# Where TensorE waits for the overflow words of a mixture of experts, and where the last tile keeps its high parts

## The chip, the core and the metric

The kernel runs on one core of one Trainium2 chip. The metric is the device time of a whole execution, in microseconds (us). The engines of the core are named as in the profile: PE is TensorE (matrix products), DVE is VectorE, ACT is ScalarE, POOL is GpSimd (which also issues DMAs and the gathers by index), SP is SyncE (which only issues DMAs here). Each engine runs its own list of instructions in order; they meet only at semaphores, which one engine or a DMA raises and another waits for.

## The reference

A decoder trunk of two layers on 512 tokens of width 1024. Each layer mixes tokens (state space, latent attention and block attention side by side, one output projection) and then runs a mixture of experts. The change lies in the experts alone:

```python
def moe_ffn(x, router_w, router_bias, w_gate, w_up, w_down):
    scores = sigmoid(t @ router_w)                  # 512 tokens, 16 experts
    ...                                             # best group of 4 experts, then the top 2 in it
    for e in range(N_EXPERTS):                      # D_MODEL 1024, D_EXPERT 512
        hid = silu(t @ w_gate[e]) * (t @ w_up[e])
        out = out + gates[:, e:e + 1] * (hid @ w_down[e])
```

The data are float32 throughout.

## The kernel before, in words

A loop over the two layers (`with nc.Fori(0, DEPTH) as L`) holds one block with a program for each engine. Each layer has the same course: norm and input projection, the mixers, the output projection, the router, then the experts, and at the end the rows of the experts are gathered back and added to x.

**Routing.** The router's scores are turned into a table: for every expert one tile of up to 128 token slots, and up to `NOV` = 7 further tiles for experts with more tokens. 17 tiles (`NTL`) always run; the rest depend on the data. PE makes the table with 8 small matmuls (L1025), DVE copies it to integers (`slot_idx`, L1844), and POOL then gathers the tokens of tile 0 and tile 1 from DRAM by these indices (L2057). DVE goes on for some twenty short steps: the places of the rows (`pos_i`), the weights of the two choices (`w12`), and last the control words `ctl` (L1863), which say how many further tiles there are and of which experts. Each of `pos_i` and `ctl` raises the semaphore `pos_dn` by one. The control words are read at the end of the 17 tiles by PE, ACT, DVE and POOL (`value_load`), and by SP for the expert of the last fixed tile.

**PE between routing and experts.** PE waits for `pos_dn` to be 2, runs `keep_warm(28)`, which is 28 matmuls of an identity into a bank that nobody reads (L781; a float32 matmul of this kind leaves two records in the trace, so 56), then turns the tokens of tile 0 (`turn_x(0, 0)`, L1034, which waits for the gather), runs `keep_warm(5)` and starts `gate_up(0)`.

**The tiles.** For every tile PE runs `gate_up` (L1048 to L1050, two products of 24 matmuls), `turn_x` of the next tile, `down` of the tile before (L1071 to L1077, 20 matmuls), and `turn_h` (L1056, which turns the hidden rows). A float32 product is made of three faster ones: weights and tokens are split into a high part (rounded by ACT: L1338 for gate and up, `down_hi`, L1377, for down) and a low part (what is left, by DVE: L1751, and `down_lo`, L1905, which writes it over the raw weights in their slot). The high parts of down live in `biasm` and `gain` (`down_hi_parts`), one set of buffers for all tiles; so `down_hi(e)` waits until `down(e - 1)` has read them (`y_ps`, 2e). The high parts of gate and up live in `mod` from column 0 to 5120 and in `actT` (`hi_parts`); they are free when `gate_up(e)` has finished (`gu_ps`, 2e + 2). Of `mod`, columns 5120 to 6144 hold the modulation that `y_out` multiplies with, and columns 0 to 2048 are loaded anew by SP behind the last `gate_up` (L717).

**The last tile (16).** PE runs `gate_up(16)`, `down(15)`, `turn_h(16)`, `down(16)`. Beside it ACT runs `silu(16)` (L1365), `h_out(16)` (L1369, L1370: the turned hidden rows out of PSUM), `down_hi(16)`; DVE runs `hidden(16)` (L1872), `y_out(15)` (L1879, two halves), `hidden_low(16)` (L1898), `down_lo(16)` (L1905, two parts) and `y_out(16)`. `down(16)` waits for `h_out`, `hidden_low`, both parts of `down_lo`, `y_out(15)` and the loaded weights. The weights of down of tile 16 are issued by SP (L684) when `down(14)` has ended.

## Time and profile before

| | us |
|---|---|
| median of 3 runs (lowest, highest) | 1593.85 (1592.6, 1597.31) |
| the profiled execution: its own time | 1589.72 |
| the profiled execution: its span, first to last instruction | 1587.7 |
| PE busy | 1382.0 (87%) |
| DVE busy | 1097.7 (69%) |
| ACT busy | 720.3 (45%) |
| POOL busy | 186.0 (12%) |
| mean granted TensorE clock | 0.916 of full speed |

Starts in the trace are counted from the first instruction. Busy times overlap, so they say only which engine is used most; which wait counts is read in each stage from the rows of the trace. The granted clock is given as a share of 2.4 GHz: 1.00 is 2.4 GHz and 0.50 is 1.2 GHz, and a value between them is the mean of a stretch that holds both. The first layer's experts run from about 463 to 788 us, the second layer's from about 1231 to 1556 us.

### The profile page before, as it was taken

To read this page: it belongs to the slowest core of one execution; us is meant where nothing else is said; L and a number is where in the kernel's file an instruction comes from. 1 tells how busy PE (TensorE), PEld (TensorE's weight loads), DVE (VectorE), ACT (ScalarE), POOL (GpSimd) and SP (SyncE) were. 2 spreads that over 40 slices of the span, in tenths; PEclk is the share of its full clock that TensorE was granted. 3 is DMA by queue.
4 is the path that set the end of the run, shared out by engine and by line. 5 is a ranking of instruction groups with operands and counts; after the bars stand their busy time and mean duration, and the time that the engine had idled before them with its cause. 6 is when DMAs were issued, how large, how long until landed. Compare 5 with 4: busy or idle time off the path is not lost. (4 is left out here: it accounts for less than half of the span.)

```text
span 1587.7 us, 17407 instructions
## 1 busy us (share of the span) xinstructions
PE 1382.0 (87%) x6479; PEld 1074.5 (68%) x6479; DVE 1097.7 (69%) x1295; ACT 720.3 (45%) x983; POOL 186.0 (12%) x268
## 2 busy tenths in 40 slices
PE   7499988987989999999618998888698999999981
PEld 3377785665777777777416777656577777777761
DVE  0577775674559888888358786666646888888862
ACT  1422433454237666666123333344513666666640
POOL 0000013400101000010020000261000100000002
PEclk9699999688999999999858999978799999999995
DMA  9536562321369999997365374243107799999944
GB/s 347 201 106 227 189 226 70 133 80 67 126 266 354 406 394 400 401 401 310 119 229 180 123 274 172 93 159 106 67 33 311 267 398 401 403 402 408 386 154 172
DMA packets 95260, 379.54 MB, mean 239 GB/s; under 512 B 5897, under 2 KB 8695, under 8 KB 85704
## 3 DMA queue, kind: packets, MB, share of 16 engines
q1 hardware_dynamic: 71592, 308.82, 51.5%
q0 software_dynamic: 15264, 55.63, 9.0%
q10 hardware_dynamic: 8320, 13.96, 2.5%
q8 instruction: 54, 0.88, 0.2%
q14 instruction: 30, 0.25, 0.0%
HBM read 345.58 MB, written 32.82 MB: 238 GB/s over the span
## 5 line engine op out<-in xcount | busy, mean ns | idle before, releaser
L1048 PE MATMUL ps<-mod_rounded,work_rounded 128*128 128x512 f32 x340 | 137.7, 405 | 2.0 <-DVE work_rounded L1885 2.0
L1050 PE MATMUL ps<-mod_rounded,work_rounded 128*128 128x512 f32 x340 | 133.8, 394 | 0.0
L1751 DVE TENSOR_TENSOR ring_rounded<-ring,mod_rounded 128x2048 fp32r<-128x2048 f32 (+1 forms) x54 | 102.9, 1930 | 23.5 <-ACT mod_rounded L1338 23.5
L1049 PE MATMUL ps<-ring_rounded,work_rounded 128*128 128x512 f32 x288 | 113.2, 393 | 0.0
L1751 DVE TENSOR_TENSOR work_rounded<-work,mod_rounded 128x2048 fp32r<-128x2048 f32 (+1 forms) x48 | 91.4, 1932 | 31.3 <-ACT mod_rounded L1338 31.3
L1431 DVE SCALAR_TENSOR_TENSOR gain<-ring,csil,gain 128x512 f32<-128x512 f32 x134 | 102.2, 763 | 4.6 <-DMA ring<-in_ada_w 1.6
L1049 PE MATMUL ps<-work_rounded 128*128 128x512 f32 x256 | 100.6, 393 | 0.0
L806 PE MATMUL ps<-ring_rounded,actT_rounded 128*128 128x512 f32 (+1 forms) x256 | 93.5, 365 | 0.0
L1338 ACT ACTIVATE mod_rounded<-ring 128x2048 fp32r<-128x2048 f32 (+1 forms) x54 | 86.2, 1631 | 0.0
L1202 ACT ACTIVATE work<-ps 128x512 f32<-128x512 f32 (+1 forms) x48 | 26.3, 548 | 127.8 <-PE ps L806 76.4
L1075 PE MATMUL ps<-biasm_rounded,work_rounded 128*128 128x512 f32 x136 | 82.2, 604 | 0.0
L1133 ACT ACTIVATE work<-x 128x1024 f32<-128x1024 f32 x16 | 16.9, 1058 | 143.7 <-DVE x L1453 70.0
L1048 PE MATMUL ps<-actT_rounded,work_rounded 128*128 128x512 f32 x204 | 81.0, 397 | 0.0
L1050 PE MATMUL ps<-actT_rounded,work_rounded 128*128 128x512 f32 x204 | 80.2, 393 | 0.0
L1358 ACT ACTIVATE work_rounded<-ps 128x512 fp32r<-128x512 f32 x68 | 36.9, 595 | 92.8 <-PE ps L1034 92.8
L806 PE MATMUL ps<-work_rounded,mod_rounded 128*128 128x512 f32 (+1 forms) x192 | 77.5, 404 | 0.0
L1338 ACT ACTIVATE mod_rounded<-work 128x2048 fp32r<-128x2048 f32 (+1 forms) x48 | 76.6, 1632 | 0.0
L923 PE MATMUL ps<-work 64*128 64x256 f32 (+7 forms) x128 | 63.3, 585 | 14.4 <-DVE sml L1705 12.3
L2057 POOL DMA_INDIRECT work<-ffn_rows,slot_idx x34 | 37.5, 1102 | 318.7 <-PE ps L1034 286.0
L1048 PEld LDWEIGHTS ps<-mod_rounded,work_rounded 128*128 128x128 f32 x340 | 63.7, 187 | 16.2 <-DVE work_rounded L1885 2.9
L1050 PEld LDWEIGHTS ps<-mod_rounded,work_rounded 128*128 128x128 f32 x340 | 63.9, 188 | 15.8
L806 PE MATMUL ps<-work_rounded,actT_rounded 128*128 128x512 f32 (+1 forms) x192 | 72.1, 376 | 0.0
(329 smaller groups left out, 3586.1 us busy)
## 6 DMA issues: line engine op xcount, KB each, us to landing
ring<-in_ada_w SPq DMA_DIRECT2D x38, 1024.0 KB, 5.3
ring<-in_moe_w_gate SPq DMA_DIRECT2D x18, 2048.0 KB, 10.0
ring<-in_moe_w_up SPq DMA_DIRECT2D x18, 2048.0 KB, 10.4
ring<-in_moe_w_down SPq DMA_DIRECT2D x18, 2048.0 KB, 11.3
work<-in_moe_w_gate SPq DMA_DIRECT2D x16, 2048.0 KB, 10.2
work<-in_moe_w_up SPq DMA_DIRECT2D x16, 2048.0 KB, 10.9
work<-in_moe_w_down SPq DMA_DIRECT2D x16, 2048.0 KB, 11.7
expert_rows<-work POOLq DMA_DIRECT2D x34, 512.0 KB, 8.3
```

Source lines behind the costliest of these rows:

```text
L806: mm = pe.matmul(ps[n % 2][:, 0:wd], h_[:, P * t:P * t + P], w_, start=first_, stop=last_)
L923: pe.matmul(ps[2 + n % 2][:, 0:P * (t + 1)], qT[0:d, h % 2, P * t:P * t + P], kT[0:d, h % 2, 0:P * (t + 1)], start=True, stop=True).then_i ...
L1048: pe.matmul(ps[j][:, :], xl, hi, start=k == 0, stop=False)
L1049: pe.matmul(ps[j][:, :], xh, lo, start=False, stop=False)
L1050: mm = pe.matmul(ps[j][:, :], xh, hi, start=False, stop=k == KD - 1)
L1075: pe.matmul(ps[6 + b][:, :], hT_lo[:, k, :], hi_[:, k - k0, cols], start=False, stop=False)
L1202: a.activation(dst, ps[n % 2][:, 0:in_width[b]], ACT.Silu if b == 0 else ACT.Copy).then_inc(win_ev, 1)
L1338: a.activation(buf, slots[3 * odd + j][:, 512 * k0:512 * k1], ACT.Copy).then_inc(w_hi, 1)
L1358: a.activation(xeT_r[:, 4 * j:4 * j + 4, :], ps[2 + j][:, :].rearrange("p (k n) -> p k n", k=4), ACT.Copy).then_inc(xt_ev, 1)
L1431: add(v.scalar_tensor_tensor(acc, w, csil[:, k:k + 1], acc, ALU.mult, ALU.add))
L1751: v.tensor_tensor(slots_r[3 * odd + j][:, 512 * k0:512 * k1], slots[3 * odd + j][:, 512 * k0:512 * k1], buf.bitcast(F32), ALU.subtract).th ...
L2057: g.indirect_dma_start(out=dst, out_offset=None, in_=hf_rows, in_offset=bass.IndirectOffsetOnAxis(ap=col, axis=0)).then_inc(sem_, 16)
```

## The change

Four edits, all in the experts of each layer.

1. PE: the wait for `pos_dn` leaves its place behind the table matmuls and stands ahead of the `value_load` of the control words, behind `down` of the last tile. ACT gets the same wait ahead of its own `value_load`.
2. PE: `keep_warm(28)` becomes `keep_warm(20)`, and `keep_warm(5)` becomes `keep_warm(4)`.
3. The high parts of down of the last tile go to `mod`, columns 2048 to 4096 and 4096 to 5120 (`down_hi_last`), and no longer to `biasm` and `gain`. `down_hi` of that tile waits for `gu_ps` = 34, the end of `gate_up(16)`, in place of `y_ps` = 32, the end of `down(15)`.
4. The order for the last tile: ACT runs `down_hi(16)` ahead of `h_out(16)`, and DVE runs `down_lo(16)` ahead of `y_out(15)` and `hidden_low(16)`.

```diff
--- before.py
+++ after.py
@@ -226,6 +226,10 @@
 
     DOWN_SPLIT = 3
     down_hi_parts = [(0, 2, biasm_r[:, :, :].rearrange("p a b -> p (a b)")), (2, 3, gain_r[:, :])]
+    down_hi_last = [(0, 2, mod_r[:, 2048:4096]), (2, 3, mod_r[:, 4096:5120])]
+
+    def down_high(e):
+        return down_hi_last if e == NTL - 1 else down_hi_parts
 
     hL = mod_r[:, 2048:6144].rearrange("p (k n) -> p k n", k=KD)
     in_hi = [view(s0 + 2048 * n, 2048, of=work_r) for n in range(3)] + [mod_r[:, 0:2048]]
@@ -1024,7 +1028,6 @@
                 for m in range(2 * T):
                     mm = pe.matmul(ps[3][:, 0:NT], row_oh[:, m, :], tile_tok[:, m, :], start=m == 0, stop=m == 2 * T - 1)
                 mm.then_inc(tab_ps, 1)
-                pe.wait_ge(pos_dn, 2)
 
 
                 def turn_x(e, odd):
@@ -1069,7 +1072,7 @@
                     for b in range(2):
                         cols = slice(512 * b, 512 * b + 512)
                         pe.matmul(ps[6 + b][:, :], hT3, w[:, 3, cols], start=True, stop=False)
-                        for k0, k1, buf in down_hi_parts:
+                        for k0, k1, buf in down_high(e):
                             hi_ = buf.rearrange("p (k n) -> p k n", k=k1 - k0)
                             for k in range(k0, k1):
                                 pe.matmul(ps[6 + b][:, :], hT_lo[:, k, :], hi_[:, k - k0, cols], start=False, stop=False)
@@ -1078,9 +1081,9 @@
                                                start=False, stop=k == DOWN_SPLIT - 1)
                         mm.then_inc(y_ps, 1)
 
-                keep_warm(28)
+                keep_warm(20)
                 turn_x(0, 0)
-                keep_warm(5)
+                keep_warm(4)
                 gate_up(0, 0, first=True)
                 turn_x(1, 1)
                 turn_h(0)
@@ -1092,6 +1095,7 @@
                     turn_h(e)
                 down(NTL - 1, (NTL - 1) % 2)
 
+                pe.wait_ge(pos_dn, 2)
                 nov = pe.value_load(ctl[0:1, 0:1], min_val=0, max_val=NOV)
                 with pe.Fori(0, NOV - 1) as i:
                     with pe.If(nov > i + 1):
@@ -1371,9 +1375,11 @@
 
                 def down_hi(e, odd):
                     a.wait_ge(*expert_loaded(e, odd, 2))
-                    if e:
+                    if e == NTL - 1:
+                        a.wait_ge(gu_ps, 2 * NTL)
+                    elif e:
                         a.wait_ge(y_ps, 2 * e)
-                    for k0, k1, buf in down_hi_parts:
+                    for k0, k1, buf in down_high(e):
                         a.activation(buf, slots[3 * odd + 2][:, 1024 * k0:1024 * k1], ACT.Copy).then_inc(d_hi, 1)
 
                 def expert_turn(e, odd, first=False):
@@ -1388,8 +1394,9 @@
                 for e in range(NTL - 1):
                     expert_turn(e, e % 2, first=e == 0)
                 silu(NTL - 1)
+                down_hi(NTL - 1, (NTL - 1) % 2)
                 h_out(NTL - 1)
-                down_hi(NTL - 1, (NTL - 1) % 2)
+                a.wait_ge(pos_dn, 2)
                 nov = a.value_load(ctl[0:1, 0:1], min_val=0, max_val=NOV)
                 with a.Fori(0, NOV - 1) as i:
                     with a.If(nov > i + 1):
@@ -1899,7 +1906,7 @@
                                     ALU.subtract).then_inc(hl_lo, 1)
 
                 def down_lo(e, odd):
-                    for m, (k0, k1, buf) in enumerate(down_hi_parts):
+                    for m, (k0, k1, buf) in enumerate(down_high(e)):
                         v.wait_ge(d_hi, 2 * e + (m + 1))
                         cols = slice(1024 * k0, 1024 * k1)
                         v.tensor_tensor(slots_r[3 * odd + 2][:, cols], slots[3 * odd + 2][:, cols], buf.bitcast(F32),
@@ -1915,9 +1922,9 @@
                     hidden_low(e)
                     down_lo(e, e % 2)
                 hidden(NTL - 1)
+                down_lo(NTL - 1, (NTL - 1) % 2)
                 y_out(NTL - 2, (NTL - 2) % 2)
                 hidden_low(NTL - 1)
-                down_lo(NTL - 1, (NTL - 1) % 2)
                 y_out(NTL - 1, (NTL - 1) % 2)
                 v.wait_ge(y_ev, 2 * NTL)
                 v.wait_ge(pos_dn, 2)
```

On PE, behind the routing, this stood before (the names in brackets are the semaphores that an instruction waits for: `slot_selectors_done` is `sel_dn`, `positions_done` is `pos_dn`, `tokens_gathered0` is `gat[0]`, `expert_tokens_low_done` is `xl_dn`):

```order
L1025 MATMUL ps<-work_rounded 128x24 [waits slot_selectors_done]
L1025 MATMUL ps<-work_rounded 128x24 x7
L781 MATMUL ps<-cst 128x128 [waits positions_done]
L781 MATMUL ps<-cst 128x128 x27
L1034 MATMUL ps<-cst,work 128x128 [waits tokens_gathered0]
L1034 MATMUL ps<-cst,work 128x128 x7
L781 MATMUL ps<-cst 128x128 x5
L1048 MATMUL ps<-mod_rounded,work_rounded 128x512 [waits weights_low_done,expert_tokens_low_done]
```

and this stands there now:

```order
L1029 MATMUL ps<-work_rounded 128x24 [waits slot_selectors_done]
L1029 MATMUL ps<-work_rounded 128x24 x7
L785 MATMUL ps<-cst 128x128 x20
L1037 MATMUL ps<-cst,work 128x128 [waits tokens_gathered0]
L1037 MATMUL ps<-cst,work 128x128 x7
L785 MATMUL ps<-cst 128x128 x4
L1051 MATMUL ps<-mod_rounded,work_rounded 128x512 [waits weights_low_done,expert_tokens_low_done]
```

The fill of 28 became 20 and follows the table matmuls without a wait; the wait now stands ahead of the load of the control words at the end of the tiles.

On ACT, in the last tile, this stood before, from `silu(16)` to the control words (`hidden_transposed` is `ht_ps`, `expert_out_in_psum` is `y_ps`, `gate_up_in_psum` is `gu_ps`):

```order
L1365 ACTIVATE work<-ps 128x512 [waits hidden_done,gate_up_in_psum]
L1369 ACTIVATE work_rounded<-ps 128x384 [waits hidden_transposed]
L1370 ACTIVATE work<-ps 128x128
L1377 ACTIVATE biasm_rounded<-ring 128x2048 [waits expert_out_in_psum,slot2_loaded]
L1377 ACTIVATE gain_rounded<-ring 128x1024
L1393 TENSOR_LOAD ctl
```

and this stands there now:

```order
L1369 ACTIVATE work<-ps 128x512 [waits hidden_done,gate_up_in_psum]
L1383 ACTIVATE mod_rounded<-ring 128x2048 [waits gate_up_in_psum,slot2_loaded]
L1383 ACTIVATE mod_rounded<-ring 128x1024
L1373 ACTIVATE work_rounded<-ps 128x384 [waits hidden_transposed]
L1374 ACTIVATE work<-ps 128x128
L1400 TENSOR_LOAD ctl [waits positions_done]
```

The two big copies moved ahead of `h_out`, write to `mod`, and wait for `gate_up` where they waited for `down`.

On DVE, in the last tile, this stood before, from `hidden(16)` to the load of the control words (`down_weights_high_done` is `d_hi`, `hidden_columns_out` is `ht_ev`):

```order
L1872 TENSOR_TENSOR work<-ps,work 128x512 [waits hidden_transposed,gate_up_in_psum,gate_silu_done]
L1879 TENSOR_TENSOR work<-ps,mod 128x512 [waits expert_out_in_psum,expert_out_stored1]
L1879 TENSOR_TENSOR work<-ps,mod 128x512 [waits expert_out_in_psum]
L1898 TENSOR_TENSOR work_rounded<-ps,work_rounded 128x384 [waits hidden_columns_out]
L1905 TENSOR_TENSOR ring_rounded<-ring,biasm_rounded 128x2048 [waits down_weights_high_done]
L1905 TENSOR_TENSOR ring_rounded<-ring,gain_rounded 128x1024 [waits down_weights_high_done]
L1879 TENSOR_TENSOR work<-ps,mod 128x512 [waits expert_out_in_psum,expert_out_stored0]
L1879 TENSOR_TENSOR work<-ps,mod 128x512 [waits expert_out_in_psum]
L1924 TENSOR_LOAD ctl [waits positions_done,expert_out_scaled]
```

and this stands there now:

```order
L1879 TENSOR_TENSOR work<-ps,work 128x512 [waits hidden_transposed,gate_up_in_psum,gate_silu_done]
L1912 TENSOR_TENSOR ring_rounded<-ring,mod_rounded 128x2048 [waits down_weights_high_done]
L1912 TENSOR_TENSOR ring_rounded<-ring,mod_rounded 128x1024 [waits down_weights_high_done]
L1886 TENSOR_TENSOR work<-ps,mod 128x512 [waits expert_out_in_psum,expert_out_stored1]
L1886 TENSOR_TENSOR work<-ps,mod 128x512 [waits expert_out_in_psum]
L1905 TENSOR_TENSOR work_rounded<-ps,work_rounded 128x384 [waits hidden_columns_out]
L1886 TENSOR_TENSOR work<-ps,mod 128x512 [waits expert_out_in_psum,expert_out_stored0]
L1886 TENSOR_TENSOR work<-ps,mod 128x512 [waits expert_out_in_psum]
L1931 TENSOR_LOAD ctl [waits positions_done,expert_out_scaled]
```

The two differences of `down_lo(16)` moved ahead of both halves of `y_out(15)` and of `hidden_low(16)`.

## Rows read from the trace of the kernel before

**Rows 1.** Groups of PE by line and form: busy us, mean ns | idle before, releaser.

```profile
L1048 PE MATMUL ps<-mod_rounded,work_rounded 128*128 128x512 f32 x340 | 137.7, 405 | 2.0 <-DVE work_rounded L1885 2.0
...
L781 PE MATMUL ps<-cst 128*128 128x128 f32 x332 | 44.9, 296 | 7.8 <-DVE ctl L1863 7.8
...
L1071 PE MATMUL ps<-ring,work 128*128 128x512 f32 x72 | 38.8, 622 | 12.2 <-DVE ring_rounded L1905 12.2
```

**Rows 2.** Timeline, layer 1, routing to tile 0: start, duration, what [idle before].

```profile
444.51 4.71 PE L781 MATMUL ps<-cst 128*128 128x128 f32 x40
...
449.74 1.06 PE L1025 MATMUL ps<-work_rounded 128*128 128x24 f32 x8 [0.52 <-DVE work_rounded L1839]
...
451.89 1.05 POOL L2057 DMA_INDIRECT work<-ffn_rows,slot_idx  x1 [16.11 <-DVE slot_idx L1844]
...
454.58 2.27 DVE L1751 TENSOR_TENSOR ring_rounded<-ring,mod_rounded 128x2048 fp32r<-128x2048 f32 x1
...
454.72 8.40 PE L781 MATMUL ps<-cst 128*128 128x128 f32 x56 [3.91 <-DVE ctl L1863]
...
462.96 1.04 PE L1034 MATMUL ps<-cst,work 128*128 128x128 f32 x8
```

**Rows 3.** DMA issues of 451.5 to 452.5 us, with median us to landing.

```profile
work<-ffn_rows,slot_idx POOLq DMA_INDIRECT x1, 6.1
```

**Rows 4.** The same, of 1218 to 1219.9 us, layer 2.

```profile
work<-ffn_rows,slot_idx POOLq DMA_INDIRECT x1, 6.6
```

**Rows 5.** Timeline, layer 2, routing to tile 0.

```profile
1219.29 1.05 POOL L2057 DMA_INDIRECT work<-ffn_rows,slot_idx  x1 [16.06 <-DVE slot_idx L1844]
...
1230.64 1.04 PE L1034 MATMUL ps<-cst,work 128*128 128x128 f32 x8
```

**Rows 6.** Stretches: length, busy of PE, PEld, DVE, ACT, POOL, granted clock, DMA share, GB/s.

```profile
455.00:459.00 4.00, 4.00 (x21) 4.00 (x22) 1.86 (x1) 0.00 (x0) 0.00 (x0) 0.54 0.69 273
305.00:308.50 3.50, 3.50 (x13) 2.04 (x11) 2.25 (x5) 1.06 (x2) 3.15 (x5) 0.50 0.00 0
987.50:991.00 3.50, 3.50 (x20) 3.50 (x20) 1.93 (x3) 0.51 (x3) 0.00 (x0) 0.54 0.00 0
```

**Rows 7.** Timeline of PE, mixers of layer 2, ahead of the third stretch.

```profile
986.44 2.49 PE L878 MATMUL ps<-work 128*128 128x64 f32 x16 [1.47 <-DVE work L1627]
```

**Rows 8.** Timeline, layer 1, last tile.

```profile
766.72 1.02 PE L1071 MATMUL ps<-work 128*128 128x512 f32 x2
766.98 0.69 DVE L1872 TENSOR_TENSOR work<-ps,work 128x512 f32<-128x512 f32 x1 [4.89 <-issue]
...
772.78 0.69 DVE L1879 TENSOR_TENSOR work<-ps,mod 128x512 f32<-128x512 f32 x1 [2.17 <-PE ps L1077]
773.22 0.49 ACT L1369 ACTIVATE work_rounded<-ps 128x384 fp32r<-128x384 f32 x1 [11.29 <-PE ps L1056]
...
773.76 1.91 ACT L1377 ACTIVATE biasm_rounded<-ring 128x2048 fp32r<-128x2048 f32 x1
...
773.90 0.56 DVE L1898 TENSOR_TENSOR work_rounded<-ps,work_rounded 128x384 fp32r<-128x384 f32 x1 [0.43 <-ACT work L1370]
775.56 1.06 ACT L1377 ACTIVATE gain_rounded<-ring 128x1024 fp32r<-128x1024 f32 x1
775.70 2.29 DVE L1905 TENSOR_TENSOR ring_rounded<-ring,biasm_rounded 128x2048 fp32r<-128x2048 f32 x1 [1.24 <-ACT biasm_rounded L1377]
777.91 1.22 DVE L1905 TENSOR_TENSOR ring_rounded<-ring,gain_rounded 128x1024 fp32r<-128x1024 f32 x1
...
779.28 2.05 PE L1071 MATMUL ps<-ring,work 128*128 128x512 f32 x2 [6.10 <-DVE ring_rounded L1905]
...
787.18 0.69 DVE L1879 TENSOR_TENSOR work<-ps,mod 128x512 f32<-128x512 f32 x1 [2.17 <-PE ps L1077]
```

**Rows 9.** DMA issues of 755 to 756 us, with us to landing.

```profile
ring<-in_moe_w_down SPq DMA_DIRECT2D x1, 2048.0 KB, 10.7
```

**Rows 10.** Timeline: when that load was issued.

```profile
755.29 0.38 SPq L684 DMA_DIRECT2D ring<-in_moe_w_down  x1
```

## The prediction

> **What bounds the kernel now.** I read the views in this order: the groups of PE, the timeline of the stretch between routing and tile 0, the landing of the gathers, the timeline of the last tile, and the granted clock of a few short stretches. The reader is to see first that between its two ends the expert stage is bound by PE: the first product of a whole gate and up, 340 matmuls over both layers, was kept waiting for 2.0 us in all [rows 1]. So nothing inside the tiles can be won or lost by moving copies on ACT or DVE, and only the stage's two ends are open. Both show as idle time of PE in the same view: 7.8 us at L781 until DVE has written `ctl`, and 12.2 us at L1071 until DVE has made the low weights of down [rows 1]. Two layers share these, 3.9 and 6.1 us each [rows 2, 8]. The change goes for exactly these two waits.
>
> **The start of the experts, layer 1.** PE ends the table matmuls at 449.74 + 1.06 = 450.80, idles 3.91, and then fills from 454.72 to 462.96, when `turn_x(0)` follows without a pause [rows 2]. What `turn_x(0)` really needs is the gather: issued at 451.89, landed 6.1 later, 457.99 [rows 2, 3]. So before, the fill ran 5.0 us past the landing. Now the fill starts at 450.80. Its length: 40 records took 4.71 us where the clock was full [rows 2], and 20 matmuls are 40 records, so it ends at 455.5, before the landing. `turn_x(0)` starts at about 458.1 (a tenth for the release), 4.9 us earlier. In layer 2 the gather lands at 1219.29 + 6.6 = 1225.9, so `turn_x(0)` moves from 1230.64 to 1226.0, 4.6 us earlier [rows 4, 5]. Sum 9.5. What follows hangs on `turn_x(0)` at the same distances: the shorter second fill, 8 records instead of 10, still ends ahead of `xeL`. The cover that stands by: DVE's first low weights are done at 454.58 + 2.27 = 456.85 [rows 2], so DVE is free when `x_low(0)` comes; the steps that write `ctl` keep their time and PE reads `ctl` over 300 us later, so the moved wait costs nothing there, and neither does ACT's. Nobody else is queued behind them.
>
> Here the Trainium skill can be held against a row. The row: this gather took 6.1 us from issue to landing [rows 3]. The page "DMA: Bandwidth & Descriptors", section "Anatomy of one DMA — SWDGE (gpsimd) path", has a fixed 2.0 us and bytes by 436e3 per us; for half a megabyte that makes an estimate of 3.2 us, which the trace doesn't bear out. What it would give is a rival below.
>
> **What the clock takes back at the start.** PE now idles from 455.5 to 458.1, 2.6 us, and in layer 2 about 3.0 (there the gather's issue, 1219.29, again 1.09 behind the end of the table matmuls, puts that end at 1218.2 and the end of the fill at 1222.9). Before, the 3.9 us of idling brought the clock down: it was 0.54 over 455 to 459, during the fill [rows 6], where it hurt nobody. Gaps shorter than the new one do it too: 1.47 us idle ahead of 986.44 was followed by a clock of 0.54 from 987.5 to 991, with PE busy throughout [rows 6, 7]. So I take it that the clock falls in this gap, or just behind it, and that `turn_x`, the small fill and the first products of tile 0 meet half of it. Bounds: zero, if it does not fall; above, what a fallen clock cost a dense `down`: `down(16)` took 787.18 - 779.28 = 7.90 from its first matmul to the release of DVE, `down(15)` 772.78 - 766.72 = 6.06, so 1.84 [rows 8]. The low stretch partly lies in the gap and beside `x_low`'s chain, so I take 1.0 a layer. Start of both layers: 9.5 - 2.0 = 7.5.
>
> **The end of the experts.** Before, from `turn_h(16)`, which ends at 779.28 - 6.10 = 773.18, a chain of five steps kept PE idle: `h_out` 773.22, the first copy of `down_hi` 773.76 to 775.67, DVE's difference 775.70 to 777.99, the second difference to 779.13, PE 779.28 [rows 8]. Now the copies wait for `gate_up(16)` only. It ended when DVE's `hidden` started, 766.98. The other thing they wait for is the load, landed at 755.29 + 10.7 = 765.99, 1 us earlier [rows 9, 10]. So ACT copies from 767.0 to 768.9, and, as the second started 1.80 behind the first, to 769.9. DVE: `hidden` until 767.67, wait, first difference 768.95 to 771.24, second to 772.4. All of this lies beside `down(15)` on PE, 766.72 to 772.6. What is late next: `y_out(15)`, whose second half needs the end of `down(15)`, 772.78, and takes 0.69, so 773.5; `h_out`, unchanged, 773.22 to 773.87; `hidden_low` 773.90 to 774.46. `down(16)` follows 0.15 later, as it did: 774.6 instead of 779.28, 4.7 us earlier. The first half of `y_out(15)` is 2.5 us later than before, which only its own bank feels, and that bank is needed at 774.6. POOL's store of tile 15 waits for both halves and starts up to 0.5 later; its landing is needed by nobody before the last gather.
>
> The clock gives something on top: the gap shrinks from 6.10 to 774.6 - 773.18 = 1.4 us. If the clock stays up, `down(16)` takes 6.06 and not 7.90: 1.84 more. The gap lies just under the 1.47 after which it fell [rows 7], so I count it as staying up in about two of three ends and take 1.2 a layer (bounds 0 and 1.84). The page "TensorE: Matmul & The Clock Gate", section "What's actually happening", says the monitor runs freely and is not started by the kernel, so how many matmuls are slow varies from run to run; the sum would be the same, and it is why this term is a share and not yes or no. End: 2 × (4.7 + 1.2) = 11.8. Behind `down(16)` stand the store, the gathers of the rows and the barrier, all of which hang on it, so the gain goes through to the end of the layer. Layer 2 repeats these rows (12.2 for two waits [rows 1]).
>
> **The sum.** 7.5 + 11.8 = 19.3 us. The profiled execution took 1589.72 (span 1587.7), so it would take 1570.4. The median of the runs is 1593.85, 4 us above the profiled one; 1593.85 - 19.3 = 1574.5, which I give.
>
> **Rivals.**
> - The clock never falls at the new gaps. For it: the same stretches are dense otherwise. Against: rows 6 and 7. Gain 9.5 + 9.4 + 3.7 = 22.6: 1571.3.
> - The gather lands earlier than it did, since the price of 6.1 comes from sharing the queues with the last weight loads, and that share could turn out smaller. At 3.2 after issue it would land at 455.1, within the fill, `turn_x(0)` starts at the end of the fill, 455.5 and 1222.9, and the clock has no gap to fall in. Start 7.5 + 7.7 = 15.2, with the end's 11.8 a gain of 27.0: 1566.9. The page of the skill named above gives the 3.2. Against: nothing that the gather shares is moved by the change.
> - The end gives less, because the load of the last down weights has only 1.0 us of slack now where it had 7.8. If it lands 3 us later in an ordinary run, the differences end at 774.4, `y_out(15)` follows to 775.7 and pushes `hidden_low` to 776.3: `down(16)` at 776.4, gain 2.9 in place of 4.7 and the longer gap drops the clock: 2 × (1.8 + 1.2) = 6 less, 1580.5.
> - The clock stays low for long. From 305 to 308.5 it was 0.50 with PE busy throughout [rows 6]. If it stayed low for some 13 us behind each start, that costs 6.5 a layer in place of 1.0: gain 8.3, 1585.5. For it: that row. Against: that was in the mixers with their small matmuls, and behind the gap in front of `down(16)` it came back within the tile.
> - Slower than before: the same mechanism, in the first tiles of both layers, with its price: each us at half clock costs 0.5 us of PE-bound work. Without the clock's cost the gain is 21.3, so it turns at 43 us of low clock in all, 21 a layer, more than a tile. At 30 us a layer it costs 30: 1602.5. Against: no dense stretch of the rows shows it.
>
> **How the numbers follow.** Forecast 0.73 (own range 1570 to 1579, from the clock bounds and 2 us of scatter of a median); clock never falls 0.13; earlier gather 0.02; late load 0.07; long low clock 0.03; slower 0.02. About 0.3%, 5 us, is what a measurement of this kernel can tell from no change. Faster by more: all but the last two, 0.95; the long low clock can end within it, 0.03; slower 0.02. The range 1567 to 1581.5 leaves out the last two, the earlier gather at its edge, and the rest's own tails.
>
> **What would show it.** After the table matmuls PE must go into 40 records of fill with no idle time, and `turn_x(0)` must begin within 0.2 of the gather's landing, some 7.3 us after the table matmuls' end (before: 12.2). L781 must lose its wait for `ctl`. In the last tile the copies L1377 must start beside `down(15)`, the wait of L1071 must be about 1.4 us and be released by `hidden_low` and no longer by `down_lo`. It is wrong if the wait of L1071 is over 3 us, if the first tile after `turn_x(0)` takes over 3 us longer than before, or if another wait of PE appears in the tiles between.

## The result

| | before | changed |
|---|---|---|
| median (lowest, highest), us, 4 runs each | 1595.58 (1592.6, 1598.45) | 1572.11 (1570.04, 1574.24) |
| profiled execution, its own time | 1589.72 | 1572.55 |
| its span | 1587.7 | 1570.7 |
| mean granted clock | 0.916 | 0.919 |

The ratio changed to before is 0.9874, 95% interval 0.9845 to 0.9903: 1.3% faster, which is 20.1 us by the ratio (15 to 25 by its interval). Forecast were 1574.5 us and a gain of 19.3. The medians are 23.5 us apart and the profiled executions 17.2.

### The profile after

The waits of PE in the expert stage of layer 1, 440 to 800 us (who waited for whom, us in total, times, longest); layer 2 has the same four:

```profile
PE ps L1037 <- DMA work<-ffn_rows,slot_idx: 3.1, 1, 3.1
PE ps L1074 <- DVE work_rounded L1905: 1.4, 1, 1.4
PE ps L1059 <- DVE work L1879: 1.2, 1, 1.2
PE ps L1051 <- DVE work_rounded L1892: 0.5, 1, 0.5
```

The wait for `ctl` (3.9 us a layer, [rows 1]) is gone, and the 6.1 us ahead of `down(16)` have become 1.4, now released by L1905, `hidden_low`. A new wait stands at L1037, `turn_x(0)`: 3.1 us for the gather.

The start of layer 1, to be laid beside [rows 2] (start, duration, what [idle before]):

```profile
451.96 1.06 PE L1029 MATMUL ps<-work_rounded 128*128 128x24 f32 x8 [0.51 <-DVE work_rounded L1846]
...
452.87 4.71 PE L785 MATMUL ps<-cst 128*128 128x128 f32 x40
...
454.11 1.05 POOL L2064 DMA_INDIRECT work<-ffn_rows,slot_idx  x1 [16.11 <-DVE slot_idx L1851]
...
460.71 1.23 PE L1037 MATMUL ps<-cst,work 128*128 128x128 f32 x8 [3.13 <-DMA work<-ffn_rows,slot_idx]
...
461.74 1.92 PE L785 MATMUL ps<-cst 128*128 128x128 f32 x8
...
463.38 0.80 PE L1051 MATMUL ps<-mod_rounded,work_rounded 128*128 128x512 f32 x1
...
464.82 0.46 PE L1051 MATMUL ps<-mod_rounded,work_rounded 128*128 128x512 f32 x1
```

The fill follows the table matmuls without a pause and takes the 4.71 us that 40 records take at the full clock. `turn_x(0)` begins within 0.1 of the gather's landing, which came 6.6 us after its issue here and 6.5 in layer 2:

```profile
work<-ffn_rows,slot_idx POOLq DMA_INDIRECT x1, 6.6
```

The second fill (8 records in 1.92) and the first products (0.80, 0.63) are slow; the product that starts at 465.12 takes the full clock's 0.40.

The last tile of layer 1, beside [rows 8]:

```profile
765.25 1.02 PE L1074 MATMUL ps<-work 128*128 128x512 f32 x2
765.50 0.69 DVE L1879 TENSOR_TENSOR work<-ps,work 128x512 f32<-128x512 f32 x1 [4.90 <-issue]
765.51 2.87 ACT L1383 ACTIVATE mod_rounded<-ring 128x2048 fp32r<-128x2048 f32 x2 [5.06 <-PE ps L1053]
...
767.46 3.43 DVE L1912 TENSOR_TENSOR ring_rounded<-ring,mod_rounded 128x2048 fp32r<-128x2048 f32 x2 [1.26 <-ACT mod_rounded L1383]
...
770.80 1.28 DVE L1886 TENSOR_TENSOR work<-ps,mod 128x512 f32<-128x512 f32 x2
...
771.74 0.49 ACT L1373 ACTIVATE work_rounded<-ps 128x384 fp32r<-128x384 f32 x1 [3.37 <-PE ps L1059]
...
772.43 0.56 DVE L1905 TENSOR_TENSOR work_rounded<-ps,work_rounded 128x384 fp32r<-128x384 f32 x1 [0.34 <-ACT work L1374]
...
773.09 1.10 PE L1074 MATMUL ps<-ring,work 128*128 128x512 f32 x2 [1.39 <-DVE work_rounded L1905]
...
779.24 0.69 DVE L1886 TENSOR_TENSOR work<-ps,mod 128x512 f32<-128x512 f32 x1 [2.18 <-PE ps L1080]
```

Both copies and both differences now lie beside `down(15)`; `down(16)` takes 779.24 - 773.09 = 6.15 us to the release of DVE, in place of 7.90.

The granted clock in short stretches (length, busy of PE, PEld, DVE, ACT, POOL, clock, DMA share, GB/s):

```profile
462.00:465.00 3.00, 3.00 (x12) 2.69 (x12) 2.97 (x4) 0.58 (x1) 0.94 (x1) 0.51 0.35 111
1218.00:1221.00 3.00, 3.00 (x14) 2.90 (x14) 2.19 (x3) 1.20 (x2) 0.94 (x1) 0.50 0.11 19
1215.80:1222.60 6.80, 5.73 (x22) 5.25 (x23) 3.79 (x4) 1.20 (x2) 0.94 (x1) 0.51 0.32 113
1234.00:1236.00 2.00, 0.67 (x5) 0.43 (x5) 2.00 (x5) 2.00 (x3) 0.95 (x1) 1.00 0.83 299
1236.00:1240.00 4.00, 4.00 (x11) 3.15 (x12) 3.15 (x2) 4.00 (x4) 0.00 (x0) 0.57 0.98 409
```

The first two are the falls behind the gap at `turn_x(0)`. The third row shows how long the second one lasted: the clock stayed low for 6.8 us in layer 2, and for about half of that in layer 1, where the product at 465.12 met the full clock. The last row is a fall that the prediction does not have. It came in layer 2 of this execution, behind `turn_h(0)`, with PE busy in all of the stretch. PE always idles twice there, once ahead of `turn_h(0)` and once right behind it:

```profile
1234.80 0.66 PE L1059 MATMUL ps<-cst,work 128*128 128x128 f32 x4 [1.21 <-DVE work L1879]
1235.99 0.51 PE L1051 MATMUL ps<-mod_rounded,work_rounded 128*128 128x512 f32 x1 [0.54 <-DVE work_rounded L1892]
```

Since the two layers start at different times in every execution, the runs are best compared on a scale of their own. This table is worked out from the timelines: us from the end of the table matmuls to each mark, layer 1 / layer 2.

| run | `turn_x(0)` starts | `turn_h(0)` starts | `turn_h(16)` ends | `down(16)` starts | last `y_out` starts |
|---|---|---|---|---|---|
| before | 12.16 / 12.39 | 28.21 / 28.45 | 322.38 / 322.50 | 328.48 / 328.60 | 336.38 / 336.70 |
| changed | 7.69 / 7.62 | 24.52 / 25.55 | 318.68 / 321.27 | 320.07 / 322.65 | 326.22 / 328.82 |
| start alone | 7.61 / 7.53 | 24.45 / 24.36 | 318.60 / 318.70 | 324.70 / 324.80 | 332.73 / 332.80 |
| end alone | 12.43 / 12.07 | 28.48 / 28.12 | 322.64 / 322.18 | 324.02 / 323.57 | 330.18 / 329.74 |
| fill of 32 | 7.62 / 7.67 | 23.78 / 23.77 | 317.93 / 317.93 | 319.31 / 319.31 | 325.47 / 325.48 |
| gather first | 6.35 / 5.42 | 22.46 / 21.53 | 318.36 / 315.58 | 319.74 / 316.97 | 325.92 / 323.14 |
| fills shorter, nothing else | 10.37 / 10.48 | 26.42 / 26.53 | 322.05 / 322.35 | 328.15 / 328.45 | 336.20 / 336.49 |
| DVE's old order | 7.50 / 7.53 | 24.33 / 24.36 | 318.38 / 318.62 | 323.15 / 323.39 | 331.91 / 332.06 |
| old buffers | 7.79 / 7.64 | 24.62 / 24.48 | 318.68 / 318.83 | 325.47 / 325.63 | 333.29 / 333.33 |
| gather first, gaps filled | 5.71 / 5.66 | 21.86 / 21.77 | 315.92 / 315.94 | 317.31 / 317.33 | 323.46 / 323.48 |
| changed, again | 7.62 / 7.80 | 24.46 / 24.63 | 318.50 / 318.88 | 319.89 / 320.27 | 326.05 / 326.42 |
| gather first, gaps filled, again | 5.66 / 5.51 | 21.81 / 21.62 | 316.16 / 315.77 | 317.55 / 317.16 | 323.70 / 323.32 |

The last column shortened by 10.16 and 7.88 us, 18.0 in all, of which 17.2 show in the profiled executions' own times. In the second profile of the changed kernel it shortened by 10.33 and 10.28, 20.6 in all. What lies outside this stretch varies by itself: the table matmuls of layer 1, ahead of everything that the change touches, ended at 450.80 before and at 453.02 after. So a median moves by a few us for reasons that are not the change's, and the verdicts below rest on this table and on the waits, the medians being the check.

### The profile page after: what moved, and what is told of

Its sections match the earlier page's. It is cut to its first block and busy times, and to the rows that moved or that the text cites. A ratio compares the mean times of both kernels' runs of the same rounds, so it can differ in the third digit from the quotient of the medians.

```text
span 1570.7 us, 17335 instructions
## 1 busy us (share of the span) xinstructions
PE 1379.1 (88%) x6443; PEld 1072.3 (68%) x6443; DVE 1097.4 (70%) x1295; ACT 721.0 (46%) x983; POOL 184.8 (12%) x268
## 5 line engine op out<-in xcount | busy, mean ns | idle before, releaser
L1078 PE MATMUL ps<-biasm_rounded,work_rounded 128*128 128x512 f32 x128 | 75.8, 592 | 0.0
## 6 DMA issues: line engine op xcount, KB each, us to landing
ring<-in_moe_w_up SPq DMA_DIRECT2D x18, 2048.0 KB, 10.8
```

Of the source, the lines that this page charges most:

```text
L1078: pe.matmul(ps[6 + b][:, :], hT_lo[:, k, :], hi_[:, k - k0, cols], start=False, stop=False)
```

## The experiments

Medians of each group of runs stand beside those of the kernel before in the same rounds.

### The two halves apart

Start alone:

```diff
--- kernel before
+++ start alone
                 mm.then_inc(tab_ps, 1)
-                pe.wait_ge(pos_dn, 2)
...
-                keep_warm(28)
+                keep_warm(20)
                 turn_x(0, 0)
-                keep_warm(5)
+                keep_warm(4)
...
                 down(NTL - 1, (NTL - 1) % 2)
 
+                pe.wait_ge(pos_dn, 2)
                 nov = pe.value_load(ctl[0:1, 0:1], min_val=0, max_val=NOV)
...
+                a.wait_ge(pos_dn, 2)
                 nov = a.value_load(ctl[0:1, 0:1], min_val=0, max_val=NOV)
```

> The start alone: the kernel before with PE's (and ACT's) wait for the control words moved behind the last tile and the fills 20 and 4; the last tile as it was. Theory 1 (the two ends add up, the start gives 4.7 us a layer less what a fallen clock takes back): in the changed kernel's trace the start gave 3.7 us in layer 1 and only 1.2 in layer 2, so 4 to 8 us in all, 0.3 to 0.5% faster than before; idle of PE at turn_x(0) about 3.1 us, released by the gather; the wait of down(16) still 6.1. Theory 2 (the start is worth nothing, the whole 20 us came from the last tile): within 2 us of before. Theory 3 (the clock costs nothing): 9.5 us faster.

Measured: 1579.66 us against 1591.3, ratio 0.9938 (0.9914 to 0.9962), 9.9 us faster by the ratio. In the table 3.65 and 3.90, 7.5 in all. The waits of PE, by group, over both layers:

```profile
L1070 PE MATMUL ps<-ring,work 128*128 128x512 f32 x72 | 38.8, 622 | 12.2 <-DVE ring_rounded L1906 12.2
...
L1033 PE MATMUL ps<-cst,work 128*128 128x128 f32 x272 | 36.7, 280 | 6.0 <-DMA work<-ffn_rows,slot_idx 6.0
```

Theory 1 stands: 3 us a layer for the gather, 6.1 at `down(16)` as before. Theory 2 is out by the interval. The 9.9 us of the ratio are more than the 4 to 8 of theory 1, but its interval (6.0 to 13.7 us) reaches below 8, and the table's 7.5 lies within them. Theory 3 (9.5) lies inside that interval too, but not in the table, and the clock fell behind the gap of both layers.

End alone:

```diff
--- kernel before
+++ end alone
+    down_hi_last = [(0, 2, mod_r[:, 2048:4096]), (2, 3, mod_r[:, 4096:5120])]
...
-                    if e:
+                    if e == NTL - 1:
+                        a.wait_ge(gu_ps, 2 * NTL)
+                    elif e:
                         a.wait_ge(y_ps, 2 * e)
...
                 silu(NTL - 1)
+                down_hi(NTL - 1, (NTL - 1) % 2)
                 h_out(NTL - 1)
-                down_hi(NTL - 1, (NTL - 1) % 2)
+                a.wait_ge(pos_dn, 2)
...
                 hidden(NTL - 1)
+                down_lo(NTL - 1, (NTL - 1) % 2)
                 y_out(NTL - 2, (NTL - 2) % 2)
                 hidden_low(NTL - 1)
-                down_lo(NTL - 1, (NTL - 1) % 2)
```

> The end alone: the kernel before with only the last tile's edits (high parts of down to mod, down_hi ahead of h_out on ACT, down_lo ahead of y_out on DVE); PE waits for the control words behind the table matmuls, fills 28 and 5. Theory 1: 11.8 to 13.2 us faster than before (4.7 of wait and up to 2 of clock in each layer), wait of down(16) 1.4 us, wait for ctl 3.9 us. Theory 2 (the start carries at least half of the gain): under 10 us faster.

Measured: 1579.88 against 1591.3, ratio 0.9932 (0.9907 to 0.9957), 10.8 us faster by the ratio; in the table 6.20 and 6.96, 13.2 in all. The gap is 1.38 us in both layers, `down(16)` takes 6.16, and the wait for `ctl` is 3.9 as before. By the table theory 1 holds; the medians do not tell 11.8 from 10. The two halves add up: 7.5 + 13.2 = 20.7 in the table, where the changed kernel has 20.6 in its second profile and 18.0 in its first, and 1.3% of time by the ratios, which is the change's 1.3%. What the first profile lacks is told below.

### Is the idle time at the start what costs the clock?

```diff
--- changed kernel
+++ fill of 32
-                keep_warm(20)
+                keep_warm(32)
                 turn_x(0, 0)
```

> The changed kernel with a first fill of 32 in place of 20, which at the full clock is 7.4 us and should end just where the gather lands (7.6 us behind the table matmuls). Theory 1 (the idle 3.1 us in front of turn_x(0) brings the clock down and that costs 1 us or more a layer): idle at turn_x(0) under 0.5 us, clock 1.00 through gate_up(0), 2 to 4 us faster than the changed kernel, 22 to 25 faster than before. Theory 2 (the fall costs nothing, since it lies beside the chain of the tokens): the same as the changed kernel within 1 us, or up to 1 slower for a fill that overshoots the landing.

Measured: 1569.96 against 1591.3, ratio 0.9887 (0.9846 to 0.9928), with single runs from 1562.8 to 1584.42. By the ratio this is 18 us (11.5 to 24.5) in place of the 22 to 25 expected, and too scattered to set against the changed kernel, so a gain in the total is not shown. The timeline of PE says more (layer 1):

```profile
453.67 7.39 PE L785 MATMUL ps<-cst 128*128 128x128 f32 x64
461.44 1.09 PE L1037 MATMUL ps<-cst,work 128*128 128x128 f32 x8 [0.38 <-DMA work<-ffn_rows,slot_idx]
462.37 1.06 PE L785 MATMUL ps<-cst 128*128 128x128 f32 x8
464.11 0.50 PE L1051 MATMUL ps<-mod_rounded,work_rounded 128*128 128x512 f32 x1 [0.68 <-DVE work_rounded L1892]
```

and the clock over both stages:

```profile
453.00:780.00 327.00, 322.11 (x1474) 253.01 (x1473) 269.66 (x220) 202.34 (x183) 27.79 (x33) 1.00 0.89 352
1207.00:1533.00 326.00, 321.21 (x1466) 252.21 (x1466) 269.49 (x220) 202.33 (x183) 27.74 (x33) 1.00 0.89 352
```

`turn_x(0)` starts where it did, 7.6 us behind the table matmuls, the idle time is 0.38, the second fill takes 1.06 in place of 1.92, and `turn_h(0)` comes at 23.78 and 23.77 in place of 24.52 and 25.55 (24.46 and 24.63 in the second profile of the changed kernel). So the fall at the start costs 0.7 to 0.9 us in three of these four layers and 1.8 in the one where the clock stayed low for longer. That is theory 1 in its mechanism, but three of the four are under its price of 1 us or more.

### Why the gather takes 6.5 us

```diff
--- changed kernel
+++ gather first
-                for j in range(3):
+                for j in range(2):
                     load_expert(3 + j, j, 1)
                 sp.wait_ge(*read_by_pe("out", 1))
+                sp.wait_ge(gat[0], 16)
                 load_expert(2, 2, 0)
+                load_expert(5, 2, 1)
```

> The changed kernel with the loads of the down weights of tiles 0 and 1 issued by SP only when the gather for tile 0 has landed; they used to be in the DMA queues until 457 us, beside the gather. Theory 1 (the gather's 6.1 to 6.6 us are queueing behind those loads): it lands 3.2 to 4.3 us after its issue, within or at the end of the fill of 20, idle at turn_x(0) under 0.7 us, no fall of the clock there: 3 to 4 us a layer faster than the changed kernel, 26 to 28 us faster than before; the loads land some 10 to 11 us later than the gather, ahead of down_hi(0), which comes 18 us after it. Theory 2 (the 6 us are the gather's own, by its 128 rows and the issue by POOL): landing still about 6 after issue, time as the changed kernel. Theory 3 (the late loads then hold up down_hi(0)): a new wait of ACT on that load and no gain.

Measured: 1568.24 against 1591.3, ratio 0.9857 (0.9833 to 0.9881), 22.8 us faster than before by the ratio. Landing of the first gather of layer 1, and of layer 2 (us from issue):

```profile
work<-ffn_rows,slot_idx POOLq DMA_INDIRECT x1, 5.2
```

```profile
work<-ffn_rows,slot_idx POOLq DMA_INDIRECT x1, 4.3
```

With the 4 MB of down weights held back the gather lands 1.3 and 2.2 us sooner, so that much of its time came from those loads, and theory 2 is out. How much of the remaining 5.2 and 4.3 us is the gather's own is not shown: the second gather is issued 1.4 us behind it, and the DMA engines were still 0.57 and 0.48 busy in that time, in place of 0.95. Theory 1's landing of 3.2 to 4.3 is met at its upper end in layer 2 and missed in layer 1; its idle time under 0.7 us at `turn_x(0)` was missed in both (1.8 and 0.85), though the clock did not fall there; and for the 26 to 28 us that it gave for the total the ratio says 22.8 (18.9 to 26.6). Theory 3 is out: PE's waits in the tiles are the same. Layer 2 became 323.14, 5.7 under the changed kernel's 328.82. Layer 1 won at the start (22.46 at `turn_h(0)`) and lost 1.85 again in the tiles, where the clock stood at 0.71 over four us behind the idle times at `turn_h(0)`:

```profile
472.00:476.00 4.00, 2.26 (x12) 1.59 (x10) 3.92 (x5) 3.96 (x4) 1.08 (x1) 0.86 0.99 424
476.00:480.00 4.00, 4.00 (x15) 3.14 (x14) 3.24 (x1) 4.00 (x5) 0.00 (x0) 0.71 1.01 420
```

That is the fall seen in layer 2 of the changed kernel, now in layer 1.

By the fit of the Trainium skill's page "DMA: Bandwidth & Descriptors", section "Anatomy of one DMA — SWDGE (gpsimd) path", the estimate for this gather was 3.2 us. Even with the weights held back the trace does not agree, at 4.3 to 5.2, though the second gather was in flight beside it.

### Is it the wait or the length of the fill?

```diff
--- kernel before
+++ fills shorter, nothing else
-                keep_warm(28)
+                keep_warm(20)
                 turn_x(0, 0)
-                keep_warm(5)
+                keep_warm(4)
```

> The kernel before with only the fills shortened to 20 and 4; PE's wait for the control words stays behind the table matmuls, the last tile as before. Theory 1 (it is the moved wait that counts, the fill only has to end near the landing): the 40 records start 3.9 us behind the table matmuls with the clock down, take some 6.2 us, and turn_x(0) starts about 10.2 us behind the table matmuls where before it was 12.2 to 12.4, so 2 us a layer, 4 in all, 0.25% faster than before, with no wait for the gather (landed at 7.2). Theory 2 (the shorter fill leaves the clock down when the tile starts): gate_up(0) slow for a while, and the gain is gone, within 1 us of before. Theory 3 (the fill is the whole of the start's gain): 7.5 us faster, as the start alone.

Measured: 1591.33 against 1591.5, ratio 0.9999 (0.9975 to 1.0024). None of the three as written. `turn_x(0)` did start 1.8 and 1.9 us earlier:

```profile
454.75 6.61 PE L781 MATMUL ps<-cst 128*128 128x128 f32 x40 [3.92 <-DVE ctl L1863]
461.20 1.04 PE L1034 MATMUL ps<-cst,work 128*128 128x128 f32 x8
```

and at full clock, as theory 1 had it, since 40 records still bring the clock up (6.61 us for them, 8.40 for 56 in [rows 2]). But in both layers the clock then fell behind `turn_h(0)`, and the tiles gave back 1.5 and 1.8 (295.6 and 295.8 us from `turn_h(0)` to the end of `turn_h(16)`, before 294.2 and 294.1):

```profile
479.00:483.00 4.00, 4.00 (x12) 3.12 (x11) 3.15 (x2) 4.00 (x5) 0.00 (x0) 0.57 0.93 389
1250.00:1254.00 4.00, 4.00 (x12) 3.09 (x11) 3.16 (x2) 4.00 (x5) 0.00 (x0) 0.58 0.96 398
```

So theory 2's result came, by a fall at another place than it had named. What holds for the change: the shorter fill without the moved wait showed no gain, though theory 1's 4 us lie right at the edge of the interval, and theory 3 is out.

### Which part of the last tile's edits is needed

DVE's order put back, the rest as changed:

```diff
--- changed kernel
+++ DVE's old order
                 hidden(NTL - 1)
-                down_lo(NTL - 1, (NTL - 1) % 2)
                 y_out(NTL - 2, (NTL - 2) % 2)
                 hidden_low(NTL - 1)
+                down_lo(NTL - 1, (NTL - 1) % 2)
```

> The changed kernel with DVE's order of the last tile put back: y_out(15), hidden_low(16), then down_lo(16); buffers in mod and ACT's order stay. Theory 1 (buffers and both orders are needed together): down_lo starts only behind hidden_low, 1.3 us behind turn_h(16), and takes 3.5, so the gap in front of down(16) is 4.9 us in place of 1.4, the clock falls (down(16) 7.9 in place of 6.2), 5 us a layer slower than the changed kernel, 8 to 12 us faster than before. Theory 2 (the buffers alone bring it, since the copies are done early): gap 1.4 to 2 us, time as the changed kernel.

Measured: 1581.06 against 1591.5, ratio 0.9933 (0.991 to 0.9956), 10.7 us faster than before. The waits of PE in layer 1:

```profile
PE ps L1074 <- DVE ring_rounded L1912: 4.8, 1, 4.8
PE ps L1037 <- DMA work<-ffn_rows,slot_idx: 2.9, 1, 2.9
```

The gap is 4.8 us and `down(16)` takes 8.76 and 8.67, more than the 7.9 expected, since more of it meets the fallen clock. It starts at 775.51, and the clock is low for 5.5 us of it; before the change it was 3.7 us (779.3 to 783). The granted clock here:

```profile
775.50:781.00 5.50, 5.49 (x11) 3.69 (x12) 0.00 (x0) 0.00 (x0) 0.00 (x0) 0.50 0.00 0
```

That is 5.7 and 5.8 us more than layer 1 of the changed kernel (326.22). Against the start alone (332.73 and 332.80) it is 0.8 us a layer less; this is what the new buffers and ACT's new order bring without DVE's. Theory 1.

The old buffers, the rest as changed:

```diff
--- changed kernel
+++ old buffers
     def down_high(e):
-        return down_hi_last if e == NTL - 1 else down_hi_parts
+        return down_hi_parts
...
-                    if e == NTL - 1:
-                        a.wait_ge(gu_ps, 2 * NTL)
-                    elif e:
+                    if e:
                         a.wait_ge(y_ps, 2 * e)
```

> The changed kernel with the last tile's high parts back in biasm and gain, and so down_hi(16) waiting for down(15), while the new orders on ACT and DVE stay. Theory 1: the copies start when down(15) ends, 0.5 us ahead of the end of turn_h(16), h_out follows them (about 3 us later than now), DVE does down_lo first, then y_out(15) and hidden_low(16): gap 6.5 to 7 us, down(16) slow at 7.9, 7 us a layer slower than the changed kernel, 4 to 8 us faster than before, which is the start's gain less up to 2. Theory 2 (the order is what counts): gap under 4 us.

Measured: 1584.81 against 1591.5, ratio 0.9954 (0.9935 to 0.9974), 7.3 us faster than before. The last tile of layer 1:

```profile
769.98 1.91 ACT L1381 ACTIVATE biasm_rounded<-ring 128x2048 fp32r<-128x2048 f32 x1 [10.92 <-PE ps L1080]
...
771.92 2.29 DVE L1910 TENSOR_TENSOR ring_rounded<-ring,biasm_rounded 128x2048 fp32r<-128x2048 f32 x1 [7.11 <-ACT biasm_rounded L1381]
772.74 0.47 ACT L1373 ACTIVATE work_rounded<-ps 128x384 fp32r<-128x384 f32 x1
...
775.27 1.28 DVE L1884 TENSOR_TENSOR work<-ps,mod 128x512 f32<-128x512 f32 x2
776.47 0.55 DVE L1903 TENSOR_TENSOR work_rounded<-ps,work_rounded 128x384 fp32r<-128x384 f32 x1
...
777.11 2.04 PE L1074 MATMUL ps<-ring,work 128*128 128x512 f32 x2 [6.79 <-DVE work_rounded L1903]
```

The copies wait for `down(15)`, `h_out` (L1373) stands behind them, and `hidden_low` (L1903) behind `down_lo` and `y_out`: a gap of 6.8 us, 0.7 more than before the change. Theory 1: the new orders pay only with the new buffers; alone it costs 0.5 us a layer against the start alone.

### A version that is faster

Gather first, a first fill of 24, and fills of an unused bank in PE's later gaps:

```diff
--- gather first
+++ gather first, gaps filled
-                def keep_warm(count):
+                def keep_warm(count, bank=7):
...
-                        pe.matmul(ps[7][:, 0:P], ident, ident, start=True, stop=True)
+                        pe.matmul(ps[bank][:, 0:P], ident, ident, start=True, stop=True)
...
-                keep_warm(20)
+                keep_warm(24)
                 turn_x(0, 0)
...
                 turn_x(1, 1)
+                keep_warm(5, 5)
                 turn_h(0)
+                keep_warm(2, 5)
...
+                keep_warm(6, 5)
                 down(NTL - 1, (NTL - 1) % 2)
```

> A version meant to beat the changed kernel: the down weights of tiles 0 and 1 loaded behind the gather (landing then 4.3 to 5.2 us after issue), first fill 24, and fills of an unused bank in PE's later gaps: 5 and 2 matmuls around turn_h(0), 6 behind turn_h(16). Theory 1 (the clock's falls at the start and at the 1.2 us gap at turn_h(0), 1.6 to 1.8 us each in the changed kernel's layer 2 and in the run with the gather first, are all avoided): from the end of the table matmuls to the last y_out 323 us in both layers (changed kernel 326.2 and 328.8), clock 1.00 throughout, 26 to 28 us faster than before. Theory 2 (the added fills delay what is behind them as much as the clock costs): 325 or more in both layers, no faster than the run with the gather first.

Measured: 1564.0 against 1591.5, ratio 0.9825 (0.9795 to 0.9856), 27.9 us faster than before by the ratio. The table has 323.46 and 323.48, the 323 of theory 1. The start of layer 1, and the clock over both stages:

```profile
448.48 5.61 PE L787 MATMUL ps<-cst 128*128 128x128 f32 x48
454.34 1.09 PE L1039 MATMUL ps<-cst,work 128*128 128x128 f32 x8 [0.25 <-DMA work<-ffn_rows,slot_idx]
457.00 0.50 PE L1053 MATMUL ps<-mod_rounded,work_rounded 128*128 128x512 f32 x1 [0.68 <-DVE work_rounded L1897]
```

```profile
448.00:776.00 328.00, 322.94 (x1482) 254.09 (x1481) 269.71 (x220) 202.34 (x183) 28.42 (x34) 1.00 0.91 359
1206.00:1530.00 324.00, 322.45 (x1478) 253.60 (x1477) 269.37 (x220) 202.34 (x183) 27.80 (x33) 1.00 0.92 362
```

The clock is 1.00 throughout, the gap at the start 0.25, and the fills hold nothing up: 294.1 us from `turn_h(0)` to the end of `turn_h(16)`, what the undisturbed layers of the other kernels have.

Beside it, the changed kernel itself, without an edit:

> The changed kernel itself once more, on the chip and in the rounds of the next run, for a comparison side by side and a second profile. Theory 1 (the clock's falls at small gaps are a matter of chance from run to run; the waits are not): idle at turn_x(0) 3.1 and in front of down(16) 1.4 again in both layers, while the stretch from the end of the table matmuls to the last y_out lies between 325.5 and 329 and need not repeat 326.2 and 328.8; 17 to 23 us faster than before. Theory 2 (the 2.6 us between the layers have a fixed cause): 326.2 and 328.8 again within 0.3.

> The version with the gather first and the gaps filled once more, beside the changed kernel. Theory 1: 323.5 in both layers again, 5 to 8 us faster than the changed kernel in the same rounds. Theory 2 (its lead over the changed kernel was another chip's state): medians within 3 us of each other.

Measured in the same rounds: the changed kernel 1570.79 (ratio 0.9856, 0.9823 to 0.989), the faster version 1565.64 (0.9839, 0.9808 to 0.987), kernel before 1590.12. The medians are 5.2 us apart and in the table the stages are 5.4 us shorter, but by the ratios it is only 2.7 us, and the intervals overlap. So the lead is shown in the stage and only likely in the total, and the 5 to 8 us that were expected are not shown there. For the changed kernel theory 1 holds: waits of 3.1 and 3.2 at `turn_x(0)` and 1.4 again, stages of 326.05 and 326.42, 22.9 us by the ratio, and no fall at `turn_h(0)`. The 328.82 of the first profile was that fall, 1.7 us, and the longer low clock at the start of the same layer, 1.1 us more than in layer 1.

## Why the prediction was right, point by point

- **The start's shift** (4.9 and 4.6 us). `turn_x(0)` came 4.47 and 4.77 earlier. In layer 1 the gather took 6.6 and not the 6.1 of [rows 3], which is the 0.4 that lacks. That the fill ends ahead of it, at 4.7, held to a tenth.
- **The clock at the start** (1.0 a layer). At `turn_h(0)` the lead was 3.69 and 2.90, so it took back 0.78 and 1.87. Of the ten profiled layers with a gap of 2.9 us or more, nine need 16.83 us from `turn_x(0)` to `turn_h(0)` in place of 16.05, so 0.8; the tenth is the one with 1.87, where the clock stayed low for 6.8 us. The size was a little high for nine layers and half of the tenth, and the fill of 32 shows the mechanism.
- **The end's shift** (4.7 a layer). The gap is 1.39 and 1.38, released by `hidden_low`; `down(16)` came 4.71 and 4.72 earlier in relation to `turn_h(16)`. The chain that the prediction named as late next, `h_out` and `hidden_low`, is what the wait now ends on, and `y_out(15)` ended before it.
- **The clock at the end** (1.2 a layer). It stayed up in all 10 profiled layers in which the 1.4 us gap was left open, so the term is 1.75 and 1.93 and not two thirds of it. The prediction had set 1.4 beside the 1.47 of [rows 7], taken the two as alike and hedged. In the trace before the 1.47 did not stand alone: PE had also idled 0.70 us shortly ahead of it, at 983.87:

```profile
983.87 1.10 PE L863 MATMUL ps<-work 128*128 128x256 f32 x4 [0.70 <-DVE work L1611]
```

The 1.4 in front of `down(16)` follows a tile without idle time. So that row was weak evidence for a fall, and the share of two thirds came from it.
- **Missed:** the clock's fall at `turn_h(0)` in layer 2 of the profiled execution, 1.67 us (295.72 against 294.05 from `turn_h(0)` to the end of `turn_h(16)`). The prediction had no term for it. The waits of 1.2 and 0.5 us there stood before the change too, with the clock up in both layers of that profile. This fall appears in 4 of the 24 layers profiled, two of them in the run with nothing but shorter fills. Why it falls in these and not in others was not settled.
- **The sum.** 3.69 + 2.90 - 1.67 + 9.43 + 3.68 = 18.0, forecast 19.3. That it is so close is in part luck: the clock gave 1.3 more at the end than the forecast had, and took 0.7 more at the start and 1.67 at `turn_h(0)`. In the second profile, without that fall, the stages gained 20.6.
- **The rivals.** "The clock never falls" is refuted by the stretches 462 to 465 and 1218 to 1221. "The gather lands earlier" did not happen by itself, but has a kernel of truth: 1.3 and 2.2 us of its 6.6 and 6.5 come from the loads beside it. "The load comes late" did not happen: the copies started with the end of `gate_up(16)`. The long low clock and the slowdown did not occur.

## What to carry to other kernels

A wait on an in-order engine should stand where the value is used; here a word needed 300 us later kept TensorE from filling and starting. Before such a wait is moved, look at what else it guards: here bank 3, which `turn_x(0)` overwrites, is read only for `slot_idx`, and the gather waits for that. When a copy waits only for its own buffer, look for one that is free earlier, and move what depends on it in the same step on every engine: of 6.6 us a layer, the buffers and ACT's order with DVE's old order gave 0.8, and the orders without the buffers lost 0.5. A fill should end where the awaited data lands, and what the data queues behind is worth a look before the fill is tuned.

## What the runs showed of the hardware

- The same gather by index of 128 rows of 4 KB landed 6.1 to 6.7 us after its issue in the 18 profiled layers in which the loads of 2 MB of down weights were still landing beside it (the DMA engines 0.95 busy in the changed kernel), and 4.3 to 5.2 us in the 6 layers in which they were held back (0.57 and 0.48 busy in the run with the gather first).
- Idle gaps of 2.9 to 3.2 us in front of `turn_x(0)` brought TensorE from 2.4 to 1.2 GHz in all 10 layers that had one; the one of 1.8 us there (gather first, layer 1) did not; gaps of 1.4 us in front of `down(16)` did in none of 10. At `turn_h(0)`, where 1.2 us of idling are followed by 0.5 us more, the clock fell in 4 of the 20 layers in which they were left open, and each such fall cost the tiles 1.5 to 1.9 us. So the length of one gap does not tell whether the clock falls: two short ones close together did it where a single longer one did not. Why they did in only 4 of the 20 stays open.
